# Two joints between products: the next product's first four weight tiles taken one token tile after the other

## The reference

```python
for i in range(DEPTH):                       # i = 0: GLA, i = 1: MLA
    h = rms_norm(x, g_pre)
    y = mixer(h, *params)                    # its last step is "... @ w_out", 2048 wide
    x = x + rms_norm(y, g_post)
# third block: h = rms_norm_2(x, norm1_w); proj = h @ w_in
```

## Time and profile before

| | |
|---|---|
| span of the profiled execution | 2344.7 us |
| its time | 2346.51 us |
| PE busy | 2302.2 us (98%) |
| VectorE busy | 1468.6 us (63%) |
| ScalarE busy | 1298.4 us (55%) |
| mean granted TensorE clock | 0.996 |
| joint 1: PE's last matmul ahead of it, first tile k behind it | 410.43, 416.44 us |
| joint 2: the same | 769.91, 775.74 us |

### The profile page before, as it was taken

The page is one execution under the profiler, slowest core; times in us unless marked ns, Lnnn a source line. Parts: engine busy times, 40 slices in busy tenths (PEclk is TensorE's granted clock), DMA queues, the critical chain, the costliest instruction groups (busy, mean ns, idle before and its releaser), DMA issues.

```text
span 2344.7 us, 32560 instructions
## 1 busy us (share of the span) xinstructions
PE 2302.2 (98%) x12152; PEld 1941.0 (83%) x12152; DVE 1468.6 (63%) x2548; ACT 1298.4 (55%) x2374; POOL 18.4 (1%) x38
## 2 busy tenths in 40 slices
PE   8999999999999999999999999999999999999998
PEld 7877888788888888867888888888888888888886
DVE  4554565665665666867777666756566566665554
ACT  5644555666555545755556546546555555554444
POOL 1000000000000000000000000000000000000000
PEclk9999999999999999999999999999999999999999
DMA  7555566565445555665453326555666666665554
GB/s 230 166 166 148 172 202 197 152 183 170 134 142 191 154 180 179 186 191 168 137 169 115 102 81 234 198 187 178 190 189 189 189 189 189 189 207 191 192 190 164
DMA packets 232429, 409.09 MB, mean 174 GB/s; under 512 B 21505, under 2 KB 46385, under 8 KB 231889
## 3 DMA queue, kind: packets, MB, share of 16 engines
q1 hardware_dynamic: 228256, 393.07, 54.1%
q0 software_dynamic: 3152, 10.59, 1.2%
q10 hardware_dynamic: 864, 3.35, 0.4%
HBM read 400.66 MB, written 6.29 MB: 174 GB/s over the span
## 4 chain that ended last, share of the span: by engine, by line
PE 92%; ACT 3%; DVE 3%; DMA 1%; issue 1%; ACTq 0%; DVEq 0%; POOL 0%; SPq 0%; POOLq 0%
PE banks L410 51%; PE banks L374 17%; PE banks L376 8%; PE banks L404 5%; PE banks L848 1%; PE banks L688 1%; ACT weights_high L342 1%; DVE weights_low L345 1%; PE banks L2389 1%; PE banks L2400 1%; PE banks L859 0%; DMA weight_ring<-in_w_in 0%; PE banks L1214 0%; PE banks L867 0%; PE banks L868 0%
## 5 line engine op out<-in xcount | busy, mean ns | idle before, releaser
L345 DVE TENSOR_TENSOR weights_low<-weight_ring,weights_high 128x512 fp32r<-128x512 f32 x1464 | 998.1, 691 | 781.0 <-ACT weights_high L342 750.3
L342 ACT CAST weights_high<-weight_ring 128x512 fp32r<-128x512 f32 (+2 forms) x1476 | 904.6, 619 | 962.4 <-PE banks L410 597.4
L410 PE MATMUL banks<-weights_high,hidden_T 128*128 128x512 f32 x2976 | 857.4, 400 | 6.8 <-DVE weights_low L345 5.2
L410 PEld LDWEIGHTS banks<-weights_high,hidden_T 128*128 128x128 f32 x2976 | 549.3, 189 | 128.0 <-issue 11.6
L374 PE MATMUL banks<-hidden_T,weights_high 128*128 128x512 f32 x1728 | 543.3, 396 | 1.3 <-DVE weights_low L345 0.8
L410 PE MATMUL banks<-weights_low,hidden_T 128*128 128x512 f32 x1488 | 461.4, 391 | 0.0
L376 PEld LDWEIGHTS banks<-hidden_T,weights_low 128*128 128x128 f32 x1728 | 324.6, 188 | 76.7
L376 PE MATMUL banks<-hidden_T,weights_low 128*128 128x256 f32 x1728 | 339.5, 278 | 0.0
L410 PEld LDWEIGHTS banks<-weights_low,hidden_T 128*128 128x128 f32 x1488 | 280.0, 188 | 61.1
L374 PEld LDWEIGHTS banks<-hidden_T,weights_high 128*128 128x128 f32 x1728 | 263.1, 189 | 2.3 <-DVE weights_low L345 1.5
L410 PE MATMUL banks<-weights_high,ffn_high 128*128 128x512 f32 x344 | 106.3, 390 | 1.6 <-DVE weights_low L345 1.6
(11 more groups left out here) (427 smaller groups left out, 1793.8 us busy)
## 6 DMA issues: line engine op xcount, KB each, us to landing
weight_ring<-in_w_in SPq DMA_DIRECT2D x168, 512.0 KB, 3.5
weight_ring<-in_w_gla_in SPq DMA_DIRECT2D x96, 512.0 KB, 3.8
weight_ring<-in_w_gate SPq DMA_DIRECT2D x88, 512.0 KB, 3.9
weight_ring<-in_w_ffn_up SPq DMA_DIRECT2D x88, 512.0 KB, 3.8
weight_ring<-in_w_down SPq DMA_DIRECT2D x88, 512.0 KB, 3.7
weight_ring<-in_w_mla_in SPq DMA_DIRECT2D x48, 512.0 KB, 3.7
weight_ring<-in_w_gla_out SPq DMA_DIRECT2D x32, 512.0 KB, 4.4
weight_ring<-in_w_mla_out SPq DMA_DIRECT2D x32, 512.0 KB, 4.3
```

The costliest lines, as they stand in the source:

```text
L342: nc.scalar.copy(hi, raw).then_inc(high_ready, 1)
L345: nc.vector.tensor_tensor(lo, raw, hi.bitcast(F32), ALU.subtract).then_inc(low_ready, 1)
L410: last = pe.matmul(ps[:, b + t, 0:width], a[:, t * P:(t + 1) * P], w, start=(k == 0 and n_th == 0), stop=(k == kt - 1 and n_th == 2))
```

## The change

Both joints get the class `JointByToken`.

- The first four tiles k of the next product's first chunk are taken for token tile 0, then for token tile 1 (`by_token` in `Product.tensor`). At joint 1 that is the same 24 matmuls in another order. At joint 2, where tokens stream, each of the 48 matmuls with 256 columns becomes two with 128 (`multiply_half` with `turned`).
- Groups 0 and 1 are transposed and split per token tile: units 0 and 1 are groups 0 and 1 of token tile 0, units 2 and 3 the same of token tile 1, units 4 to 9 are groups 2 to 7 whole. ScalarE and VectorE work on 128x128 pieces in units 0 to 3.
- PE: units 0 and 1 ahead of (t, k) = (0, 0), units 2 and 3 ahead of (0, 2), units 4 and 5 ahead of (1, 3), units 6 and 7 ahead of k = 5, units 8 and 9 ahead of k = 7.
- VectorE and ScalarE take the steps of the joint in a new order. `add(2, ...)`, `add(3, ...)` and `gained`, which stood ahead of the split of tile k = 4 of the next product, stand now between the splits of k = 5 to 7.

The diff (shortened; both joints are made with `halves=True`, branches for `False` are left out, and so is `tensor` for k = 0, which is not reached):

```diff
-                _, kt, _, _, width, acts, _ = self.chunks[n]
+                _, kt, _, _, width, acts, turned = self.chunks[n]
...
                 ahi, alo = (a[:, t * P:(t + 1) * P] for a in acts(k))
+                if turned:
+                    for half in range(2):
+                        for w, a, n_th in ((hi, ahi, 0), (hi, alo, 1), (lo, ahi, 2)):
+                            for f in range(half * P, width, 2 * P):
+                                at = half * S + t * P
+                                last = pe.matmul(ps[:, b + f // (2 * P), at:at + P], w[:, f:f + P], a,
+                                                 start=(k == 0 and t == 0 and half == 0 and n_th == 0), stop=False,
+                                                 skip_group_check=True)
+                    return last
...
-            def tensor(self, pe, before=None, first_half=None):
+            def tensor(self, pe, before=None, first_half=None, by_token=None):
...
+                        if by_token is not None and n == 0:
+                            ahead = PARTS
+                            for t in range(NT):
+                                for k in range(PARTS):
+                                    by_token(t, k)
+                                    last = self.multiply_half(pe, i, n, k, b, t)
+                                    if t == NT - 1:
+                                        last.then_inc(split_used, 1)
                         for k in range(ahead, kt - by_halves):
                             if before is not None and isinstance(i, int) and i == 0:
                                 before(n, k)
...
+        class HalveByToken(Halve):
+                self.units = [(0, (0,)), (1, (0,)), (0, (1,)), (1, (1,))] + [(g, (0, 1)) for g in range(2, self.n)]
...
+            def turn_unit(self, pe, u):
+                g, tokens = self.units[u]
+                bank = self.banks[u % 4]
+                if u >= 4:
+                    pe.wait_ge(low_out, self.first + u - 4 + 1)
+                for kk in range(2):
+                    for t in tokens:
+                        o = kk * S + t * P
+                        last = pe.transpose(ps[:, bank, o:o + P], self.src(t, 2 * g + kk), ident)
+                last.then_inc(turned, 1)
...
+            def scalar_steps(self):
+                    nc.scalar.wait_ge(turned, self.turned0 + u + 1)
+                    for x, hi, _, gain in self.parts(u):
+                        last = nc.scalar.activation(hi, x, ACT.Copy, scale=gain)
+                    last.then_inc(high_out, 1)
+                    yield
...
+        class JointByToken(Joint):
...
+            def first_tiles(self, pe, t, k):
+                turn = self.turn
+                if (t, k) == (0, 0):
+                    pe.wait_ge(self.added, 1)
+                    turn.turn_unit(pe, 0)
+                    turn.turn_unit(pe, 1)
+                elif (t, k) == (0, 2):
+                    pe.wait_ge(self.added, 2)
+                    turn.turn_unit(pe, 2)
+                    turn.turn_unit(pe, 3)
+                elif (t, k) == (1, 3):
+                    pe.wait_ge(self.added, 4)
+                    turn.turn_unit(pe, 4)
+                    turn.turn_unit(pe, 5)
+                turn.wait_unit(pe, 2 * t + k // 2)
+            def tensor(self, pe, k):
...
+                elif k in (3, 5, 7):
+                    pe.wait_ge(self.added, k + 1)
+                    self.turn.turn_unit(pe, k + 1)
+                    self.turn.turn_unit(pe, k + 2)
+                self.turn.wait_unit(pe, 2 + k // 2)
+            def begin_scalar(self, prod, after):
...
+                self.turns = self.turn.scalar_steps()
+                act.wait_ge(first_done, self.n)
+                squares_of(0)
+                after.split(act, 0, 0, 0)
+                self.post.root(0)
+                after.split(act, 0, 0, 1)
+                prod.wait_done(act, prod.rounds - 1, n)
+                squares_of(1)
+                next(self.turns)
+                self.post.root(1)
+                next(self.turns)
...
+                after.split(act, 0, 0, 2)
+                after.split(act, 0, 0, 3)
+                if self.halves:
+                    for _ in range(3):
+                        next(self.turns)
+            def scalar(self, pace, row=False):
+                next(self.turns)
+                yield from pace.to(2)
+                yield from pace.run(self.turns)
+                for t in range(NT):
+                    yield from pace.to(7 + 3 * t)
+                    act.wait_ge(self.added, NT * D // W)
+                    Sc(act.activation(junk, X[:, t, :], ACT.Square, accum_out=self.norm.rstd[:, t:t + 1]))
...
+            def begin_vector(self, prod, after):
+                self.turns = self.turn.vector_steps()
+                self.post.inverse(0)
+                after.split(v, 0, 0, 0)
+                self.post.ready(0)
+                self.add(0, 0)
+                after.split(v, 0, 0, 1)
+                self.post.inverse(1)
+                    next(self.turns)
+                    self.post.ready(1)
+                    self.add(0, 1)
+                    next(self.turns)
+                    after.split(v, 0, 0, 2)
+                    after.split(v, 0, 0, 3)
+                    next(self.turns)
+                    next(self.turns)
+                    self.add(1, 0)
+                    self.add(1, 1)
+                    next(self.turns)
...
+            def vector(self, pace, row=False):
+                next(self.turns)
+                yield from pace.to(1)
+                self.add(2, 0)
+                self.add(2, 1)
+                yield from pace.to(2)
+                v.wait_ge(chunk_squared, NT * self.n * (D // W))
+                gained(prod, D // W - 1, 2 * ((prod.chunk0 + 1) % 2)).then_inc(chunk_evicted[(prod.chunk0 + 1) % 2], 1)
+                prod.wait_evicted(v)
+                self.add(3, 0)
+                yield from pace.to(3)
+                next(self.turns)
+                self.add(3, 1)
+                yield from pace.to(4)
+                yield from pace.run(self.turns)
...
+        joint1 = JointByToken(1, post0, norm1, "l1_pre", True)
+        joint2 = JointByToken(2, post1, norm2, "norm1", True)
...
+            prod_lat.tensor(pe, lambda n, k: joint1.tensor(pe, k) if n == 0 else None,
+                            by_token=lambda t, k: joint1.first_tiles(pe, t, k))
...
-            prod_dn.tensor(pe, turn_residual)
+            prod_dn.tensor(pe, turn_residual, by_token=lambda t, k: joint2.first_tiles(pe, t, k))
```

More of the change, by code:

```diff
@@ L747, in wait, with place, parts, wait_unit @@
                 eng.wait_ge(low_out, self.first + self.n)
+        class HalveByToken(Halve):
+            def place(self):
+                self.units = [(0, (0,)), (1, (0,)), (0, (1,)), (1, (1,))] + [(g, (0, 1)) for g in range(2, self.n)]
+                self.turned0, self.first = planned["turned"], planned["halved"]
+                planned["turned"] += len(self.units)
+                planned["halved"] += len(self.units)
+            def turn_unit(self, pe, u):
[8 more added lines that the diff above has]
+                last.then_inc(turned, 1)
+            def parts(self, u):
+                g, tokens = self.units[u]
+                c = slice(tokens[0] * P, (tokens[-1] + 1) * P)
+                for kk in range(2):
+                    k = 2 * g + kk
+                    hi, lo = self.dst(k)
+                    yield ps[:, self.banks[u % 4], kk * S + c.start:kk * S + c.stop], hi[:, c], lo[:, c], self.gain(k)
+            def wait_unit(self, pe, u):
+                pe.wait_ge(low_out, self.first + u + 1)
+            def scalar_steps(self):
+                for u in range(len(self.units)):
+                    nc.scalar.wait_ge(turned, self.turned0 + u + 1)
[3 more added lines that the diff above has]
+                    yield
+            def vector_steps(self):
+                for u in range(len(self.units)):
+                    nc.vector.wait_ge(high_out, self.first + u + 1)
+                    for x, hi, lo, gain in self.parts(u):
+                        last = nc.vector.scalar_tensor_tensor(out=lo, in0=x, scalar=gain, in1=hi.bitcast(F32),
+                                                              op0=ALU.mult, op1=ALU.subtract)
+                    last.then_inc(low_out, 1)
+                    yield
+            def wait(self, eng):
+                eng.wait_ge(low_out, self.first + len(self.units))
         class Norm:
@@ L3331, in _ @@
             gla_tensor(pe)
-            prod_lat.tensor(pe, lambda n, k: joint1.tensor(pe, k) if n == 0 else None)
+            prod_lat.tensor(pe, lambda n, k: joint1.tensor(pe, k) if n == 0 else None,
+                            by_token=lambda t, k: joint1.first_tiles(pe, t, k))
             early = mla_early_tensor(pe)
```

56 lines of the change are left out of this document (54 added, 2 removed).

## The result

The changed kernel takes 2359.84 us (median of five runs, 2359.73 to 2360.09), the kernel before 2347.35 us. The ratio is 1.0054 with a 95% interval of [1.0044, 1.0065]: slower by 12.5 us, well inside two per cent. The span of its profiled execution is 2357.7 us, 13.0 more than before.

What follows compares the result with a forecast made beforehand. PE, busy 98% of the span, was taken as the bound, with VectorE's list holding it at the joints. Joint 1 -0.2 and joint 2 +5.2 gave +5.0 us; with a mean of 2347.9, 2353 us was predicted, range 2345 to 2363.

Steps and rivals of the forecast that it cites:

- the likeliest case: Both joints: -0.2 us at joint 1 and +5.2 at joint 2, +5.0 in all, 2353 us; chance 0.54.
- the second rival: The clock falls at both joints all the same: 2.5 us more each, 2357 to 2358 us; chance 0.17.
- the first rival: Joint 2: 128-column matmuls go at the plain fp32 rate, 0.22 us instead of 0.12; +13.6, 2361.3 us; chance 0.17.
- Joint 1, -0.2 us: Joint 1: PE's early start is returned at k = 4, 5 and 7 because VectorE's list is no shorter; -0.2 us.
- T: The moment PE transposes units 4 and 5, put at 418.6 for joint 1 and 783.2 for joint 2.
- The three waits: Each joint: PE waits 1 to 1.5 us ahead of k = 4 (weight split), k = 5 and k = 7 (additions).
- VectorE's hole: VectorE idle ahead of unit 4 while it waits for PE: 1.6 us at joint 1, 5 us at joint 2.
- The last test of the prediction: Joint 1: the prediction is wrong there if k = 7 starts before 430 or after 432.
- Joint 2 at full clock, +5.2 us: Joint 2: 96 matmuls of 128 columns at 0.12 us each, then the 12.0 us chain to k = 7; +5.2 us.
- The granted clock 1.00 through both joints: Sign expected in the changed profile: no fall to half clock at joint 1 or joint 2.
- VectorE as the bound: Both joints: from T on PE waits for VectorE's queued splits, low parts, `gained` and additions; last addition at T + 11.0.

Runs made afterwards that it cites:

- e2: Changed kernel with joint 2 put back as before, so joint 1 alone changed: 2347.72 us against 2346.14 for the kernel before, ratio 1.0006.
- e3: Changed kernel with joint 1 put back as before, joint 2 alone changed: ten runs, five at 2348.55 to 2350.06 us, five at 2359.64 to 2360.85.
- e4: Changed kernel with joint 2 back at 256 columns without token order, small units and new engine order kept: 2352.36 us against 2346.14 before, ratio 1.0023.
- e11: Kernel before with the joint 1 of e7 and the joint 2 of e8 together: 2344.58 us against 2345.81, ratio 0.9995.
- e7: Changed kernel's joint 1 with VectorE's hole filled by moved work, joint 2 as before: 2344.77 us against 2346.53 for the kernel before, ratio 0.9991.
- e8: Joint 1 as before; joint 2 with 256 columns, no token order, small units, VectorE's hole filled, later transposes moved: 2347.27 us against 2346.53 before, ratio 1.0002.
- e9: Kernel before plus ten repeated low-part splits of tile 11 behind joint 2, so PE idles; 256 columns follow: 2353.57 us against 2345.81, ratio 1.0032.
- e10: Kernel before with the added splits of e9, then k = 11 to 15 as 120 matmuls of 128 columns: 2372.06 us, ratio 1.0110.
- e1: Kernel before with k = 8 to 11 of joint 2's first chunk as 96 matmuls of 128 columns: 2349.56 us against 2346.14, ratio 1.0012.
- e5: Kernel before with the first four tiles behind joint 2 as 96 matmuls of 128 columns, tile by tile: 2355.94 us against 2346.53, ratio 1.0038.
- e6: Kernel before with the first eight tiles behind joint 2 as 192 matmuls of 128 columns: 2356.47 us against 2346.53, ratio 1.0039.

## Why the prediction was right, and where it was not

The time lies in the range (2345 to 2363) and went the way forecast, within two per cent. But the likeliest case said +5.0 us and 2353, and 12.5 were measured; what happened is a mixture of the forecast and the second rival. That the number lies in the range is partly luck: the forecast's own range ended at 2357 and the second rival's at 2358. The rest, up to 2363, was there for the first rival, and its mechanism did not occur.

- **Joint 1, -0.2 us: right.** Without a fall of the clock it is -0.1 (e2). T to k = 7 was to take 12.0 us; in the changed kernel it is 420.33 to 432.33. (The prediction's own terms add up to T + 10.8 for the last addition, not to the T + 11.0 it goes on with; 11.0 were measured.) The three waits came where they were put, 1.4, 1.3 and 1.3 us. The pair of small low parts costs the 0.61 taken. VectorE's hole, put at 1.6 us, is 1.85 in e2 and 2.61 in the changed kernel, where the half clock makes PE late. The last test of the prediction, k = 7 between 430 and 432, fails by 0.15 (432.33 less 0.18), for the clock and not for the list.
- **Joint 2 at full clock, +5.2 us: right,** +4.8 in the profile of e3, with a hole of 4.86 us where 5 were put. 128 columns cost 0.112 and not the 0.12 taken; the reason given, that a stationary block of its own is loaded for each, fits, but was not tested. The first rival (0.22) is out. The Trainium skill's 81 ns ("TensorE: Matmul & The Clock Gate", Back-to-back issue gap) is not reached either: this fp32r stream takes 111 to 113.
- **The clock: wrong.** "The granted clock 1.00 through both joints" is the step that failed. It fell at both, for 3.4 us at joint 1 (+1.3) and for 17 us at joint 2 (+7 to +8). The rival for this had a chance of 0.17 and a price of 2.5 us a joint, because I let the half clock last 5 us at each; the trace of before has 6.8 and 3.4 us, with 512 and 256 columns behind the falls. That a half clock may last several times as long with the new matmuls of 128 columns was in no case of mine, and it is the largest single term of the loss. The argument that PE restarts sooner was not empty: at joint 1 the clock held in three of the five profiles with the new order (e2, e4, e11), and fell for 6.8 us in all eight with the old one.
- **VectorE as the bound: right,** shown by e2, e7 and e11 at joint 1, and at joint 2 by e4 against e8, where it costs 4 us and my expectation had 2.

Still open: why the clock fell at joint 2 in all five runs of the changed kernel (by their times and mean clocks; one was profiled) and in only five of ten of e3; and what ends a half clock in the middle of a 128-column stream. Three ends lie just behind eight transposes, one such set did not end it, and no run separates them from chance. Theory B, that idle time ahead of the stream brings the fall, fits the gap of 4.48 us in e9 and e10, each with a fall, but for the joints it is not shown: the profile of e3 has the same waits of 0.46 and 1.28 us at joint 2 without a fall as the changed kernel has with one.

## What to carry to other kernels

When PE waits for another engine's list of steps, an earlier start of PE gains nothing until that list gets shorter or its holes are filled: add up the list to the last step that PE waits for, and see what stands in the queue ahead of each step that waits for PE. Where the clock can fall in a stretch of idle time, look at which matmuls stand behind it: after the same gap it was back in 6.8 us with 256 streamed columns (e9) and not within the 25.6 us of the matmuls with 128 (e10). And price a clock fall by how long it lasts with the matmuls of the new kernel, not of the old one; several runs are needed for that, since it differs from run to run.

## What the runs showed of the hardware

- In a gapless stream of fp32r matmuls with 128 streamed columns, each with a 128x128 stationary block of its own, the granted clock stayed at 1.00 for 10.7 us (e1) and at 0.50 for 25.6 us (e10). With eight transposes between such matmuls the half clock ended after 10.2, 17.1 and 20.5 us in the profiles of e5, the changed kernel and e6. Where 256 or 512 columns stood behind a fall at a joint, it lasted 3.4 or 6.8 us in all 13 profiles.
- The Trainium skill ("TensorE: Matmul & The Clock Gate", Part 1, What's actually happening) says that sustained activity releases the throttle. e10 disagrees for this stream: from 799.7 to 829 PE was busy without a gap and got 1.2 GHz.
- Spacing of such matmuls: 0.112 us at 2.4 GHz, 0.213 at 1.2 GHz; with 256 columns 0.120 and 0.213. At half clock a matmul with 128 columns costs as much as one with 256.
